# Twelve projection slabs cut as 4 chunks x 512 columns, one slab placed among the channel transposes, and the state product first on GpSimd

## The reference, cut to what matters

```python
h = rmsnorm(x, attn_norm)
proj = h @ w_in
(q, k, v, iq, ik, iw, z, xbc, dt_raw, gate_a, gate_b) = jnp.split(proj, offs, axis=-1)
q = rope_partial(rmsnorm(q...), pos); k = ...; iq = rope_partial(iq...); ik = rope_partial(rmsnorm(ik)...)
y_attn = dsa_attention(q, k, v, iq, ik, iw)          # index scores from iq, ik choose 64 keys for each token
xbc = silu(causal_depthwise_conv(xbc, conv_w, conv_b))
xs, bs, cs = split(xbc)                              # 2048, 512 and 512 columns
y_ssd = ssd_chunked(xs, dt, A, bs, cs) + d_skip * xs # 32 heads of 64 in 4 groups
y_ssd = gated_group_rmsnorm(y_ssd, z, ssd_norm)      # y * silu(z), then a norm over groups of 512
merged = sigmoid(gate_a) * (y_attn @ w_attn_branch) + sigmoid(gate_b) * (y_ssd @ w_ssd_branch)
x = x + merged @ w_out                               # then a mixture of 32 experts
```

## Time and profile before

| | |
|---|---|
| median of 3 runs | 1382.62 us (1381.84 to 1382.67) |
| the profiled execution | 1379.86 us, its span 1378.1 us |
| busy share of the span: PE, PEld, DVE, ACT, POOL | 96%, 88%, 69%, 56%, 15% |
| granted TensorE clock, mean | 0.988 |
| transfers | 263 MB, 191 GB/s |

### The profile page before, as it was taken

How to read it: one execution, slowest core, us unless ns; L and a number is a source line. 1 busy time by engine, 2 the same in 40 slices (tenths; PEclk the granted TensorE clock), 3 DMA queues, 4 the chain that set the end, 5 groups by cost and what they waited for, 6 DMA issues and landing times.

```text
span 1378.1 us, 23083 instructions
## 1 busy us (share of the span) xinstructions
PE 1324.7 (96%) x9022; PEld 1206.4 (88%) x9022; DVE 944.8 (69%) x1369; ACT 766.2 (56%) x1150; POOL 205.6 (15%) x165
## 2 busy tenths in 40 slices
PE   9999999999989999999999998989999999999998
PEld 8999989889989999988998887979999788777876
DVE  6555575486566555566687775765666799999996
ACT  5333346565545333366465775325645677777774
POOL 1222220030001222210301313410001000202020
PEclk9999999999999999999999999999998999999999
DMA  8655544522356555544543442315455599999991
GB/s 311 212 187 186 186 142 157 183 93 93 131 156 197 183 183 184 171 135 154 184 148 123 123 154 71 100 47 180 143 169 184 212 400 365 339 367 334 370 338 52
DMA packets 73943, 263.44 MB, mean 191 GB/s; under 512 B 8320, under 2 KB 9600, under 8 KB 73728
## 3 DMA queue, kind: packets, MB, share of 16 engines
q1 hardware_dynamic: 72864, 260.39, 55.5%
q10 hardware_dynamic: 992, 1.86, 0.4%
HBM read 261.17 MB, written 1.05 MB: 190 GB/s over the span
## 4 chain that ended last, share of the span: by engine, by line
PE 69%; DVE 9%; ACT 5%; issue 2%; POOL 1%; DVEq 0%; ACTq 0%; POOLq 0%
PE bank L561 21%; PE bank L563 20%; PE bank L562 20%; DVE sb_wlo L518 3%; DVE sb_wlo L505 2%; ACT sb_Uh L636 1%; PE bank L2782 1%; PE bank L653 1%; ACT sb_aw L1729 1%; PE bank L2839 1%; DVE sb_XC L2118 1%; PE bank L741 1%; ACT sb_whi L489 0%; POOL sb_Xe L2441 0%; ACT sb_XC L1762 0%
## 5 line engine op out<-in xcount | busy, mean ns | idle before, releaser
L505 DVE TENSOR_TENSOR sb_wlo<-sb_raw,sb_whi 128x1024 fp32r<-128x1024 f32 (+2 forms) x304 | 384.0, 1308 | 166.3 <-ACT sb_whi L489 166.1
L489 ACT ACTIVATE sb_whi<-sb_raw 128x1024 fp32r<-128x1024 f32 (+3 forms) x308 | 301.9, 1030 | 227.8 <-PE bank L563 221.7
L561 PE MATMUL bank<-sb_Uh,sb_whi 128*128 128x256 f32 x1216 | 348.8, 287 | 11.5 <-DVE sb_wlo L505 4.3
L562 PE MATMUL bank<-sb_Ul,sb_whi 128*128 128x256 f32 x1216 | 345.3, 284 | 0.0
L563 PE MATMUL bank<-sb_Uh,sb_wlo 128*128 128x256 f32 x1216 | 345.1, 284 | 0.0
L561 PEld LDWEIGHTS bank<-sb_Uh,sb_whi 128*128 128x128 f32 x1216 | 234.1, 192 | 16.6 <-issue 9.2
L562 PEld LDWEIGHTS bank<-sb_Ul,sb_whi 128*128 128x128 f32 x1216 | 234.2, 193 | 0.9
L563 PEld LDWEIGHTS bank<-sb_Uh,sb_wlo 128*128 128x128 f32 x1216 | 234.2, 193 | 0.0
L561 PE MATMUL bank<-sb_whi,sb_Uh 128*128 128x256 f32 (+3 forms) x560 | 161.1, 288 | 7.1 <-DVE sb_Ul L645 5.3
L563 PE MATMUL bank<-sb_whi,sb_Ul 128*128 128x256 f32 (+3 forms) x560 | 158.5, 283 | 0.0
L562 PE MATMUL bank<-sb_wlo,sb_Uh 128*128 128x256 f32 (+3 forms) x560 | 158.5, 283 | 0.0
(11 more groups left out here) (407 smaller groups left out, 2258.5 us busy)
## 6 DMA issues: line engine op xcount, KB each, us to landing
sb_raw<-in_slabs SPq DMA_DIRECT2D x162, 512.0 KB, 4.5
sb_raw<-in_ffn_in SPq DMA_DIRECT2D x88, 512.0 KB, 4.5
sb_raw<-in_moe_in SPq DMA_DIRECT2D x50, 512.0 KB, 5.7
sb_raw<-in_ffn_out SPq DMA_DIRECT2D x44, 512.0 KB, 3.9
sb_raw<-in_moe_out SPq DMA_DIRECT2D x26, 512.0 KB, 5.8
sb_deep_free<-in_moe_in SPq DMA_DIRECT2D x16, 512.0 KB, 5.9
sb_deep_uh<-in_moe_in SPq DMA_DIRECT2D x16, 512.0 KB, 5.2
sb_deep_ul<-in_moe_in SPq DMA_DIRECT2D x16, 512.0 KB, 6.3
```

The costliest lines, as they stand in the source:

```text
L489: nc.scalar.activation(whi[:, i % NSLOT, c], raw[:, i % NSLOT, c], ACT.Copy).then_inc(S("hi_done"), 1)
L505: nc.vector.tensor_tensor(wlo[:, i % NSLOT, c], raw[:, i % NSLOT, c], whi[:, i % NSLOT, c].bitcast(F32), ALU.subtract).then_inc(S("lo_done ...
L561: pe.matmul(o, lh, rh, start=start, stop=False, skip_group_check=True)
L562: pe.matmul(o, lh, rl, start=False, stop=False, skip_group_check=True)
```

## The change

It has three parts, all in the second block.

1. **Slabs.** The pairs (q2, q3), (iq0, iq1), (z0, z1) to (z6, z7) hold the same 512 columns each as before, but cut otherwise: the first slab of a pair holds chunks 0 to 3 with 512 columns, the second chunks 4 to 7. `tiles_by_halves` accumulates over both slabs into two banks, one for each token tile, with 24 matmuls of 512 moving columns for a slab. An output is complete only at the end of the second slab, so the copies or SiLUs of both wait for that; each now reads one token tile with 512 columns.
2. **Order at the start of the state stage.** On TensorE the transposes of bs come first, then two groups of xs, then the side slab wa0, then the other six groups; in round u the side slab is that of u+1, so rounds 0 to 4 hold one. ScalarE splits slab wa2 between the SiLUs, and loads the exp table and takes the two exponentials ahead of the copies to `XS`; `BTM` is copied behind the second copy. VectorE splits wa2 ahead of `fe`. `Xd`, `Xe` and `BTM` get memory of their own, beside `XC`.
3. **GpSimd.** It waits only for the xs copies that a round reads, and makes `Xe` ahead of `Xd`, which also puts it ahead of the wait for the output of round u-2.

```diff
@@ -137,10 +137,16 @@
 
-    for i in range(4):
+    def slab_pair(names, lo):
+        for half, nm in enumerate(names):
+            add(nm, "w_in_2", lo, lo + 512, KD // 2, KD // 2 * half)
+
+    for i in range(2):
         add(f"q{i}", "w_in_2", i * 256, (i + 1) * 256)
-    for nm, lo, hi in (("k", C2_K, C2_V), ("v", C2_V, C2_IQ), ("iq0", C2_IQ, C2_IQ + 256), ("iq1", C2_IQ + 256, C2_IK)):
+    slab_pair(("q2", "q3"), 512)
+    for nm, lo, hi in (("k", C2_K, C2_V), ("v", C2_V, C2_IQ)):
         add(nm, "w_in_2", lo, hi)
+    slab_pair(("iq0", "iq1"), C2_IQ)
     out.append(("ik_dt", [("w_in_2", C2_IK, C2_Z), ("w_in_2", C2_DT, C2_GA)], 0, KD))
@@ -153,8 +159,8 @@
     gate_slab2(5)
-    for i in range(8):
-        add(f"z{i}", "w_in_2", C2_Z + i * 256, C2_Z + (i + 1) * 256)
+    for i in range(4):
+        slab_pair((f"z{2 * i}", f"z{2 * i + 1}"), C2_Z + i * 512)
     gate_slab2(6)
@@ -346,6 +352,9 @@
             pad = sb("pad", [P, P], F32, p2)
+            Xd = sb("Xd", [P, 2, 512], F32, p2)
+            Xe = sb("Xe", [P, 512], F32, p2)
+            BTM = sb("BTM", [P, SG, SN], F32, p2)
             with ExitStack() as pa:
@@ -605,6 +611,29 @@
             return last
+
+        def tiles_by_halves(names, banks, xh, xl):
+
+            for half, nm in enumerate(names):
+                i = slab_of[nm]
+                wh, wl = wslab(i, KD // 2, 512)
+                stage = fresh.pop() if fresh else None
+                for k in range(KD):
+                    if not half * KD // 2 <= k < (half + 1) * KD // 2:
+                        continue
+                    r = k - half * KD // 2
+                    if r % 2 == 0:
+                        pe.wait_ge(*reach("lo_done", 2 * i + r // 2 + 1))
+                    if stage is not None:
+                        pe.wait_ge(*reach(stage[0], k + 1))
+                    for t in range(NT):
+                        tk = slice(t * P, (t + 1) * P)
+                        last = mm3(bank[banks[t]][:, :], xh[:, k, tk], xl[:, k, tk], wh[:, r], wl[:, r], k == 0, k == KD - 1)
+                if stage is not None:
+                    fresh.append(stage)
+                last.then_inc(S("slab_used"), 1)
+            if fresh:
+                fresh.pop()
 
@@ -1650,15 +1679,15 @@
             tok = lambda b, n, at=0: bank[b].rearrange("p (t n) -> p t n", t=NT)[:, :, at:at + n]
-            outs = [(f"q{i}", i, xn[:, :, i * 256:(i + 1) * 256], 256) for i in range(4)]
+            outs = [(f"q{i}", i, xn[:, :, i * 256:(i + 1) * 256], 256) for i in range(2)]
+            outs += [(f"q{i}", i, xn[:, i % 2, 512:1024], 512) for i in (2, 3)]
             outs += [("k", 4, K2[:].rearrange("p t h d -> p t (h d)"), 256), ("v", 5, V2[:], 256),
-                     ("iq0", 6, IQ[:, :, 0:4].rearrange("p t h d -> p t (h d)"), 256),
-                     ("iq1", 7, IQ[:, :, 4:8].rearrange("p t h d -> p t (h d)"), 256),
+                     ("iq0", 6, IQ[:, 0].rearrange("p h d -> p (h d)"), 512), ("iq1", 7, IQ[:, 1].rearrange("p h d -> p (h d)"), 512),
                      ("ik_dt", 0, IKW[:], HD + IH), ("ik_dt", 0, ssm[:, 0:2], SH)]
             for nm, b, dst, n in outs:
                 hi_upto(nm)
-                used(act, nm)
-                act.activation(dst, tok(b, n, HD + IH if n == SH else 0), ACT.Copy).then_inc(S("b2_ev"), 1)
+                used(act, {"q2": "q3", "iq0": "iq1"}[nm] if nm in ("q2", "iq0") else nm)
+                act.activation(dst, bank[b][:, :] if n == 512 else tok(b, n, HD + IH if n == SH else 0), ACT.Copy).then_inc(S("b2_ev"), 1)
                 if nm == "q3":
@@ -1762,17 +1791,17 @@
                     gate2_out(3)
-
-            for j in range(8):
-                act.wait_ge(*reach("xs_tr", j + 1))
-                act.activation(XS[:, :, j * 256:(j + 1) * 256], tok(j % 4, 256), ACT.Copy).then_inc(S("xs_ev"), 1)
-            act.wait_ge(*reach("bt_tr", 1))
-            act.activation(BTM[:].rearrange("p g n -> p (g n)"), bank[4][:, :], ACT.Copy).then_inc(S("bt_ev"), 1)
+                    hi_upto("wa0")
             act.preload_act_table(ACT.Exp)
             act.wait_ge(*reach("acs", 2))
             act.activation(ssm[:, 7], ssm[:, 7], ACT.Exp).then_inc(S("ee"), 1)
             act.activation(ssm[:, 9], ssm[:, 5], ACT.Exp).then_inc(S("ee"), 1)
-            hi_upto("wa0")
+            for j in range(8):
+                if j == 2:
+                    act.wait_ge(*reach("bt_tr", 1))
+                    act.activation(BTM[:].rearrange("p g n -> p (g n)"), bank[4][:, :], ACT.Copy).then_inc(S("bt_ev"), 1)
+                act.wait_ge(*reach("xs_tr", j + 1))
+                act.activation(XS[:, :, j * 256:(j + 1) * 256], tok(j % 4, 256), ACT.Copy).then_inc(S("xs_ev"), 1)
 
@@ -1782,9 +1811,10 @@
 
+            side_out(0)
             for u in range(8):
-                if u < 6:
-                    hi_upto(f"wa{u}" if u < 4 else f"g{u}")
+                if u < 5:
+                    hi_upto(f"wa{u + 1}" if u < 3 else f"g{u + 1}")
                 for k in range(2):
@@ -1792,12 +1822,12 @@
                     act.activation(ST[:, u], bank[6][:, :], ACT.Copy).then_inc(S("st_ev"), 1)
-                if u < 6:
-                    side_out(u)
+                if u < 5:
+                    side_out(u + 1)
             act.preload_act_table(ACT.Silu)
             for c in range(8):
                 hi_upto(f"z{c}")
-                used(act, f"z{c}")
+                used(act, f"z{c | 1}")
                 if c >= 2:
@@ -2197,14 +2227,14 @@
                                   const("upto").unsqueeze(1).to_broadcast([P, SG, P]), ALU.mult).then_inc(S("cbm"), 1)
+            lo_upto("wa0")
             dve.wait_ge(*reach("ee", 1))
             dve.tensor_tensor(ssm[:, 7], ssm[:, 7], ssm[:, 0], ALU.mult).then_inc(S("fe"), 1)
-            lo_upto("wa0")
             for u in range(9):
                 if u < 8:
                     t, g = divmod(u, 4)
-                    if u < 6:
-                        lo_upto(f"wa{u}" if u < 4 else f"g{u}")
+                    if u < 5:
+                        lo_upto(f"wa{u + 1}" if u < 3 else f"g{u + 1}")
                     for k in range(2):
@@ -2244,8 +2274,8 @@
                 dve.wait_ge(*reach("y", 12))
-                v = XS[:, :, c * 256:(c + 1) * 256]
-                dve.tensor_tensor(v, v, sgh[:, c % 2].rearrange("p (t n) -> p t n", t=NT), ALU.mult).then_inc(S("yz"), 1)
+                v = XS[:, c % 2, c // 2 * 512:(c // 2 + 1) * 512]
+                dve.tensor_tensor(v, v, sgh[:, c % 2], ALU.mult).then_inc(S("yz"), 1)
             lo_upto("g6")
@@ -2430,15 +2460,15 @@
                 x3 = XS[:, t, g * 512:(g + 1) * 512].rearrange("p (h d) -> p h d", h=8)
-                pool.wait_ge(*reach("xs_ev", 8))
+                pool.wait_ge(*reach("xs_ev", 2 * g + 2))
                 pool.wait_ge(*reach("fe", 1))
-                if u >= 2:
-                    pool.wait_ge(*reach("y_mm", u - 1))
-                pool.tensor_tensor(Xd[:, u % 2].rearrange("p (h d) -> p h d", h=8), x3, per_head(ssm[:, t, hs]), ALU.mult).then_inc(S("xd"), 1)
                 if t == 0:
                     if u:
                         pool.wait_ge(*reach("st_mm", u))
                     pool.tensor_tensor(Xe[:].rearrange("p (h d) -> p h d", h=8), x3, per_head(ssm[:, 7, hs]), ALU.mult).then_inc(S("xe"), 1)
+                if u >= 2:
+                    pool.wait_ge(*reach("y_mm", u - 1))
+                pool.tensor_tensor(Xd[:, u % 2].rearrange("p (h d) -> p h d", h=8), x3, per_head(ssm[:, t, hs]), ALU.mult).then_inc(S("xd"), 1)
                 pool.tensor_tensor(x3, x3, per_head(pb("d_skip_2")[:, hs]), ALU.mult).then_inc(S("xsd"), 1)
@@ -2628,9 +2658,16 @@
                     continue
-                s_ = need(nm)
+                if nm in ("q3", "iq1"):
+                    continue
                 claim(b, "b2_ev", n + 1 if n < 8 else 10)
-                by_token(s_, b, Uh, Ul, KD, slabs[s_][2]).then_inc(S("slab_used"), 1)
+                if nm in ("q2", "iq0"):
+                    claim(b + 1, "b2_ev", n + 2)
+                if nm in ("q2", "iq0"):
+                    tiles_by_halves((nm, {"q2": "q3", "iq0": "iq1"}[nm]), (b, b + 1), Uh, Ul)
+                else:
+                    s_ = need(nm)
+                    by_token(s_, b, Uh, Ul, KD, slabs[s_][2]).then_inc(S("slab_used"), 1)
 
@@ -2735,17 +2772,30 @@
                 last.then_inc(S("cb_mm"), 1)
-            for j in range(8):
+            def side(u):
+                s_ = need(f"wa{u}" if u < 4 else f"g{u}")
+                claim(7, "side_ev", u + 1)
+                src = (OAh, OAl) if u < 4 else (Uh, Ul)
+                by_feature(s_, 7, *src, KD, 256).then_inc(S("slab_used"), 1)
+
+            def xs_turn(j):
                 pe.wait_ge(*reach("xc", 3 + j // 2))
                 claim(j % 4, "xs_ev", j + 1)
                 for t in range(NT):
                     for c in range(2):
```

(23 more changed lines are left out.)

3 lines of the change are left out of this document (removed).

## The result

The changed kernel takes 1373.89 us (median of 4 runs, 1373.25 to 1375.69), beside 1382.64 of the kernel before (median of 4, 1381.84 to 1383.18): a ratio of 0.9932, 95% interval 0.9912 to 0.9953. The forecast was 1374.9 and "faster". The profiled execution took 1374.05 us with a span of 1372.2. Lines of the changed kernel stand 6 further down than before in the shared helpers (the splits, the matmuls of a slab) and 29 to 46 further down in the parts of the second block read here.

What follows compares the result with a forecast made beforehand. TensorE's own work and its waits were taken as the bound, the largest wait being for `Xe` (7.5 us). Terms -9.6 - 2.2 + 1.95 + 1.8 + 0.3 = -7.7 us gave 1374.9 us; range 1370.6 to 1378.6.

Steps and rivals of the forecast that it cites:

- The state stage's start: State stage, first rounds: waits for `Xe` (4.52 and 3.0 us) and the low clock (2.42) go, 9.9 us saved.
- Its end: State stage, last rounds: both waits for VectorE and the low clock stay, four rounds without a slab cost 0.3 us.
- Rival 3: State stage's tail: fourth round without a slab at VectorE's pace (+2.4), clock falls a round earlier (+2.5); 1379.8 us, 8%.
- The z slabs: z stage: 24 matmuls of 512 columns take 5.49 us instead of 5.76, 0.27 a slab, 2.2 for eight.
- signs of being wrong: z stage: z pairs over 11.1 us, one of the listed signs that the prediction is wrong.
- rival 4: z stage: clock, low when z0 starts, stays low, making the kernel slower; four slabs would give 1397 us; 3%.
- z7's end: Behind the last z pair: z7's product 3.2 us later, 1.27 of slack eaten, y transposes later by 1.95 us.
- q and iq: q/iq pairs to the index scores: late squares, inverse root and VectorE's line shift all behind by +1.8 us.
- Clock: TensorE's longer gaps near 702 and 980: a fall costs up to 1.4 us, 0.3 counted for both.
- bound of 2.8: Upper bound, in us, on the clock's cost at the two gaps near 702 and 980; the lower was 0.

Runs made afterwards that it cites:

- e1: Changed kernel with all twelve slabs cut as before (256 columns), only the state stage's edits kept: 1374.34 us, ratio 0.9928.
- e2: Kernel before with only q2, q3 and iq0, iq1 as pairs: 1388.71 us, ratio 1.0037.
- e3: Kernel before with only the eight z slabs as pairs: 1382.21 us, ratio 0.9988.
- e5: Changed kernel with `Xd` ahead of `Xe` on GpSimd again: 1380.89 us, ratio 0.9971.
- e11: Changed kernel with the second slab's split ahead of the wait for the pair's end, in the z pairs alone: 1375.34 us, ratio 0.9925.
- e10: Changed kernel with the second slab's split ahead of the wait for the pair's end, in the q and iq pairs alone: 1372.21 us, ratio 0.9903.
- e6: Changed kernel with 7, 9 and 9 products of zeros in three gaps at TensorE's waits: 1374.8 us, ratio 0.9938.
- e4: Changed kernel with the second slab's split ahead of the wait for the pair's end, for q, iq and z: 1370.9 us, ratio 0.9902.
- e9: e1 with the z slabs as pairs, their second slab split ahead of the wait for the pair's end: 1369.81 us, ratio 0.9894.
- e7: Changed kernel with the side slabs back in their own rounds, wa2's split left among the SiLUs: 1382.01 us, ratio 0.999.

## Why the prediction was right, step by step

**The state stage's start, -9.9.** Shown, and larger: the front is 11.4 us shorter (73.1 to 61.7, e1 alone as well), 10.5 beside e2 and e3. The parts, from the two traces: the waits of rounds 2 and 3, 3.0 counted, 3.4 measured (and in e5); the low clock, 2.42 counted, 8.94 - 6.46 = 2.5 measured, of which 0.9 is the trace of before (1.6 in e2); the first product, 4.5 us counted, 5.5 measured (the slab's 5.7 less the 0.2 us that the product now comes later). The mis-sized number is where TensorE comes to the product: 838.9 was forecast, 15.1 us behind the stage's first product, and it was 13.8 (842.08 - 828.29). I had put 6.0 us of slab behind the moment at which TensorE stood free. But the slab takes 5.7 us (831.98 to 837.67), and the rest of the work up to the product takes 8.1 us, where it had taken 9.1: before, the transposes waited 0.43 us for a copy of ScalarE (the second sixteen start at 828.63), and all 32 of xs take 3.4 us now where they took 3.8 without that wait. In the list of waits that I read, the one for VectorE's sum stands fourth, not third; nothing hangs on it.

**Its end, +0.3.** Two waits for VectorE again, and a low clock into z0 as forecast. They are 4.1 us in place of 5.1, but so they are in e2 and e3, whose stage is the old one: what is off the second wait is on the work between the two, at the lower clock. From the first product that reads `ST` to z0's first matmul it is 22.4 us, 21.9 in the trace of before and 22.5 in e2 and e3, so +0.5 or nothing. From the first state-stage product to z0's first matmul it is 84.08 us (912.37 - 828.29), 94.95 before: -10.9 in place of -9.6. Rival 3 (the tail gives back half) did not come.

**The z slabs, -2.2.** z0 to z7 took 957.95 - 912.37 = 45.6 us, before 965.94 - 918.79 = 47.2: -1.6; beside e2, where the clock was low as long, -2.3. In full stride a pair takes 957.95 - 947.07 = 10.88 us, so 5.44 a slab where 5.49 was forecast. What is missing is the first pair, 12.9 us (925.31 - 912.37): 2.1 us go to the low clock, 1.1 before. Over 11.1 us was one of the signs of being wrong; it was met by this pair, through rival 4's low clock, which lasted 4 us into z0 and then ended. By the 2.5 ns beside a matmul's columns that the Trainium skill has ("TensorE: Matmul & The Clock Gate", section "Back-to-back issue gap") a slab would have been 5.18, and 5.24 in the old shape, a gain of 0.5; neither spacing was that, 5.44 and 5.76 a slab. The section gives that figure for a matmul in isolation, not for a stream with a weight load for each, as here.

**z7's end, +1.95.** Shown by e11. The second half of the y transposes starts 15.87 us behind z7's end, 14.02 before: +1.9. `YTl` was forecast at 15.1 and starts 14.9 behind.

**q and iq, +1.8.** The index score stands 51.4 us behind the first q copy, 49.9 before, and 51.4 in e2: +1.6, by the squares, the inverse root and VectorE's line, as forecast: measured from the first q copy, the inverse root starts 0.7 us later (671.34 and 669.41), and the `wlo` of xbc0 1.6 (688.48 and 685.66). e10 takes it away.

**Clock, +0.3 for both gaps.** Too small. The fall at the index scores costs 1.6 us (e6 takes 1.6 away between the index score and the state stage), that at the y transposes 0.5. I had argued from 5.1 us of waiting in the tail that single gaps of 2.5 us would mostly pass; one of 1.8 and one of 2.2 us with 0.4 us of work between did not, nor did the gap of 2.2 us alone in e4 and e10. My bound of 2.8 held it.

**Sum.** By the profile -10.9 - 1.6 + 1.9 + 1.6 + 2.1 = -6.9 us, as by the checkpoints, and -7.4 with the front and the tail of e2 as those of the kernel before; the forecast was -7.7. The timed medians differ by 8.75 us, with an interval of 6.5 to 12.2; the profiled executions by 5.8, as the changed one reached the first q copy 1.2 us later. The 1.4 to 1.9 us between the traces and the timed medians are not explained, and lie within that interval. The mechanism was right; that the time came out within 1 us of the forecast was luck in two ways: the errors of two terms (-1.3 in the stage, +1.8 of clock) offset each other, and the measurement itself leaves several us open.

## What to carry to other kernels

A slab of independent work moved into a wait was worth its whole length here (5.7 us), while reordering what feeds the wait can bring out another engine's lateness at the same place (here ScalarE's copies). Where two tiles complete together, put the splits of the next slabs ahead of the wait for the pair, or everything that reads the pair is late by a split. Measure a saving of less than 2 us in the stretch where it is made: what comes behind differed here by 3.4 us over fourteen traces. And take more than one trace of the kernel before: the same state stage had a front of 72.1 to 73.1 us in three traces, and the same tail took 85.9 us before and 87.3 in e2, as the clock fell a little earlier or later.

## What the runs showed of the hardware

- A matmul of 512 columns takes 0.2267 us in the z pairs and two of 256 take 0.24, 5.9% more; one fall of the clock (1.6 us) costs two thirds of what the four pairs of z save (2.3 to 2.4, e2 with e3 and e1 with e10).
- The granted clock fell in the changed kernel and e2 behind a gap of 1.8 us, 0.4 us of transposes and a gap of 2.2 us, and stayed at 1.00 with products of zeros in both (e6). It also stayed at 1.00 in e9, where the only wait at this place is one of 1.2 us, and fell in e4 and e10, where the only one is of 2.2 us (0.66 from 702 to 707 in e4).
- Behind the same first wait of the tail (2.6 us in all fourteen traces) the clock fell at three different moments: at once in e1 and e10 (the pair of products there takes 2.08 us, 1.13 in the changed kernel, and the tail is 1.6 us longer), a little later in ten, and only behind the second wait in the kernel before and e7. The second wait is 2.5 us in these two and 1.5 in the others.
- On GpSimd one and the same multiplication of 128 x 512 took 1.04 to 2.02 us, from round to round; in the changed kernel `Xe` of round 0 took 1.04, while VectorE did nothing (836.1 to 842.8), of round 1 1.66 and of round 2 1.31, both beside a `wlo` on VectorE, and of round 3 2.02, beside a `wlo` and other work. Such a `wlo` took 3.21 to 3.48 us there, and 2.35 where GpSimd stood still. That each slows the other fits these rows; no run tested it.
